# A streaming-encoder trunk: the first two weight units of a part multiplied row-wise, with a fourth weight place

## What is computed

```python
for l in range(DEPTH):
    x = layer_norm(ALPHA * x + 0.5 * swiglu(x, w_gate, w_up, w_down), ln1_g, ln1_b)   # F = 2816
    h = x @ w_in            # q, k, v of 8 stick-breaking heads, q, k, v of 8 chunked heads
    ...
    x = layer_norm(ALPHA * x + mixed @ w_out, ln2_g, ln2_b)
    x = layer_norm(ALPHA * x + 0.5 * swiglu(x, w_gate2, w_up2, w_down2), ln3_g, ln3_b)
```

## Time and profile before

| | |
|---|---|
| median of 3 runs | 1013.1 us (1012.2 to 1013.25) |
| the profiled execution's own time | 1012.61 us |
| its span, first to last instruction | 1010.8 us |
| PE busy | 997.8 us, 99% of the span |
| PEld (weight loads, beside PE) | 921.9 us, 91% |
| DVE busy | 812.4 us, 80% |
| ACT busy | 568.6 us, 56% |
| POOL busy | 26.5 us, 3% |
| HBM traffic | 185 MB, 183 GB/s |
| chain that ended last | PE 90%, DVE 5%, issue 2%, DMA 2% |

### The profile page before, as it was taken

One profiled execution on the slowest core, in us unless ns is written; L12 is line 12 of the kernel. 1 busy time (PEld: TensorE's weight loads), 2 busy tenths in 40 slices (PEclk: granted clock), 3 DMA queues, 4 the chain that ended last, 5 costly groups with the idle time before them and its releaser, 6 DMA issues.

```text
span 1010.8 us, 17930 instructions
## 1 busy us (share of the span) xinstructions
PE 997.8 (99%) x7020; PEld 921.9 (91%) x7020; DVE 812.4 (80%) x882; ACT 568.6 (56%) x616; POOL 26.5 (3%) x54
## 2 busy tenths in 40 slices
PE   6999999999999999999999999999999999999999
PEld 6899999799987999999889999997999889999997
DVE  4998885844788899886889988868457979988859
ACT  5655554557785655554465555536586756555545
POOL 2000000001100000000000000000010000000000
PEclk9999999999999999999999999999999999999999
DMA  8556545463324555464436574545523265545441
GB/s 333 207 197 251 220 172 185 160 228 127 126 83 167 209 207 212 168 219 182 176 126 208 208 290 167 210 138 198 205 84 126 87 247 196 210 177 210 169 187 59
DMA packets 34078, 185.22 MB, mean 183 GB/s; under 512 B 3824, under 2 KB 3824, under 8 KB 18928
## 3 DMA queue, kind: packets, MB, share of 16 engines
q1 hardware_dynamic: 32400, 174.60, 47.8%
q0 software_dynamic: 1488, 9.45, 2.4%
q10 hardware_dynamic: 144, 0.52, 0.2%
HBM read 183.51 MB, written 1.05 MB: 183 GB/s over the span
## 4 chain that ended last, share of the span: by engine, by line
PE 90%; DVE 5%; issue 2%; DMA 2%; ACT 1%; SPq 0%; ACTq 0%; DVEq 0%
PE bank L1064 26%; PE bank L1065 26%; PE bank L1066 26%; PE bank L1162 8%; PE bank L1126 2%; DVE w_lo L704 2%; DMA raw<-stream 2%; DVE xn L828 1%; PE bank L1119 1%; ACT w_hi L423 1%; PE bank L1308 1%; DVE soft_t L854 0%; DVE hl_lo L922 0%; ACT hl_hi L534 0%; DVE h_lo L914 0%
## 5 line engine op out<-in xcount | busy, mean ns | idle before, releaser
L1064 PE MATMUL bank<-xT_hi,w_hi 128*128 128x256 f32 x1568 | 444.7, 284 | 0.4 <-DVE w_lo L704 0.4
L1066 PE MATMUL bank<-xT_hi,w_lo 128*128 128x256 f32 x1568 | 443.9, 283 | 0.0
L1065 PE MATMUL bank<-xT_lo,w_hi 128*128 128x256 f32 x1568 | 443.9, 283 | 0.0
L704 DVE TENSOR_TENSOR w_lo<-raw,w_hi 128x2048 fp32r<-128x2048 f32 x122 | 278.5, 2290 | 73.3 <-ACT w_hi L423 73.3
L423 ACT ACTIVATE w_hi<-raw 128x2048 fp32r<-128x2048 f32 x122 | 232.7, 1911 | 130.4 <-PE bank L1066 129.2
L1064 PEld LDWEIGHTS bank<-xT_hi,w_hi 128*128 128x128 f32 x1568 | 300.7, 192 | 3.8 <-issue 0.8
L1065 PEld LDWEIGHTS bank<-xT_lo,w_hi 128*128 128x128 f32 x1568 | 300.8, 192 | 2.9
L1066 PEld LDWEIGHTS bank<-xT_hi,w_lo 128*128 128x128 f32 x1568 | 300.7, 192 | 0.0
L1064 PE MATMUL bank<-w_hi,h_hi 128*128 128x512 f32 x284 | 111.6, 393 | 0.6 <-DVE h_lo L874 0.6
L1065 PE MATMUL bank<-w_lo,h_hi 128*128 128x512 f32 x284 | 111.4, 392 | 0.0
L1066 PE MATMUL bank<-w_hi,h_lo 128*128 128x512 f32 x284 | 110.5, 389 | 0.0
(11 more groups left out here) (137 smaller groups left out, 1170.5 us busy)
## 6 DMA issues: line engine op xcount, KB each, us to landing
raw<-stream SPq DMA_DIRECT2D x110, 1024.0 KB, 4.8
raw<-stream SPq DMA_DIRECT2D x110, 512.0 KB, 4.1
lnp<-ln_gb POOLq DMA_DIRECT2D x6, 1024.0 KB, 6.0
band<-rel_band POOLq DMA_DIRECT2D x2, 1024.0 KB, 9.2
xn<-x POOLq DMA_DIRECT2D x1, 1024.0 KB, 6.7
out<-xn SPq DMA_DIRECT2D x4, 256.0 KB, 2.0
qT<-xT SPq DMA_DIRECT2D x1, 512.0 KB, 4.6
qT<-xT ACTq DMA_DIRECT2D x1, 512.0 KB, 4.8
```

Of the source, the lines that this page charges most:

```text
L704: nc.vector.tensor_tensor(w_lo[:, at(slot)], raw[:, slot, :], w_hi[:, at(slot)].bitcast(F32), ALU.subtract).then_inc(lo_ready, 1)
L1064: nc.tensor.matmul(o, w[0], x[0], start=start, stop=False, skip_group_check=again)
L1065: nc.tensor.matmul(o, w[0], x[1], start=False, stop=False, skip_group_check=again)
L1066: return nc.tensor.matmul(o, w[1], x[0], start=False, stop=stop, skip_group_check=again)
```

## The change

1. `SLOT_AT` gives four places of 2048 in `w_hi` and `w_lo`: slot 1 at 0, slot 0 at UW, slot 2 at 2 UW, and place 3, whose last 512 also serve one attention buffer (before, `sx_hi` and `sx_lo`).
2. The first two units of each part but the first of the run are split before the part begins: the first into place 3 (after an FFN) or place 1 (before the second FFN, where W_out's last unit goes to place 3), the second, from raw slot 1, into slot 0's place in two halves. `split_second_hi` and `split_second_lo` take the place of `split_first_*`, ahead of the LN. The loads' waits are as they were.
3. Both units are multiplied row-wise: x stands still, 512 columns (256 of each unit) move (`row_products`); all of token half 0, then all of half 1. The turns of half 1 stand inside half 0's products, those of half 0's first quarter inside the last y product, its second quarter's behind it. `keep_warm` is gone. `last_used` comes after half 0's products.
4. The results lie by rows: in attention q is copied to `row_out` (ACT, scaled), turned by eight transposes and copied into `qT`; in an FFN silu and gate work on halves, and h is turned by four transposes and copied into `h_pair`.
5. In those FFNs' first step the next gate and up units both come ahead of the products, and product 7 waits for the second gate.
6. LN: `x_lo` of the first two quarters ahead of the rstd steps (before, of one), and both first x_hi ahead of `rstd` of half 1. `gather` takes six additions before the gate of the last Strassen step and two behind it.
7. The last LN has no turns, x_hi or x_lo, and the load and split after the last unit are gone.

```diff
-SLOT_AT = (0, 2 * UW, UW)
+SLOT_AT = (UW, 2 * UW, 0, 3 * UW)
...
-            load(0, DEPTH * UNITS, source=DEPTH * UNITS - 1)
...
+            def split_second_hi(l, filled, after):
+                act.wait_ge(raw_ready[1], loaded(l, 1, filled))
+                act.wait_ge(unit_used, used(l, after))
+                for c, done in zip(HALVES, (first_hi, hi_ready)):
+                    nc.scalar.activation(w_hi[:, at(0, c)], raw[:, 1, c], ACT.Copy).then_inc(done, 1)
...
                 rstd(l, p, 0)
+                if count == 3 * DEPTH:
+                    rstd(l, p, 1)
+                    return
                 x_hi(count, 0)
+                x_hi(count, 1)
                 rstd(l, p, 1)
-                x_hi(count, 1)
...
+                    split_hi(l, base + 2, 2, first[2])
+                    silu_rows(r, 0, row_silu)
+                    silu_rows(r, 1, silu_done)
+                    split_hi(l, base + 3, 0, first[0] + 1, after=base + 1)
+                    first_unit_hi()
+                    act.wait_ge(row_turned, 2 * l + f)
+                    nc.scalar.activation(h_pair, bank[6][:, :].rearrange("p (c b t) -> p c b t", c=2, b=2),
+                                         ACT.Copy).then_inc(hf_done, 1)
+                    split_differences_hi(l, f, 0)
+                    act.wait_ge(row_h_done, 2 * (2 * l + f))
+                    silu(1, 2)
+                    high_h(0)
+                    split_last_parts_hi(l, f, 0)
+                    split_hi(l, base + 5, 2, first[2] + 1)
...
                 split_hi(l, base + 3 * SF + 5, 2, first[2] + 1 + SF)
+                if r < 3 * DEPTH - 2:
+                    split_hi(l, base + FFN_UNITS, 0, first[0] + FP, into=3, after=base + 3 * SF + 1)
                 act.wait_ge(hf_done, it(l, f, FP - 1) + 1)
...
-                split_first_hi(l, base + FFN_UNITS, first[0] + FP)
+                if r < 3 * DEPTH - 2:
+                    split_second_hi(l, first[1] + FP, base + 3 * SF + 3)
...
-                split_hi_at(l, ATT0 + 15)
+                split_hi(l, ATT0 + 15, 1, FILLED[ATT0 + 15], into=3, after=ATT0 + 1)
+                split_hi(l, FFN_BASE[1], 0, FILLED[FFN_BASE[1]], into=1, after=ATT0 + 12)
                 mixed_hi(l, 1, 0)
                 mixed_hi(l, 1, 1)
-                split_first_hi(l, FFN_BASE[1], FILLED[FFN_BASE[1]])
+                split_second_hi(l, FILLED[FFN_BASE[1] + 1], ATT0 + 13)
...
-                    if tb == 1:
-                        x_lo(phase(l, p + 1), (0,))
+                    if tb == 1 and phase(l, p + 1) < 3 * DEPTH:
+                        x_lo(phase(l, p + 1), (0, 1))
...
+                    weight_differences(l, f, 0, FILLED[base + 1] + 1)
+                    split_lo(l, base + 2, 2)
+                    weight_additions()
+                    gated_rows(r, 0)
+                    gated_rows(r, 1)
+                    split_lo(l, base + 3, 0)
+                    h_sums(0)
+                    split_pure_lo(l, f, 0)
+                    split_differences_lo(l, f, 0)
+                    low_h(0)
...
                 split_lo(l, base + 3 * SF + 2, 2)
+                gather(l, f, 0)
                 gated(SF, 3 * SF, bank[0])
+                gather(l, f, 1)
                 split_lo(l, base + 3 * SF + 3, 0)
-                gather(l, f, 0)
...
-                gather(l, f, 1)
                 split_lo(l, base + 3 * SF + 4, 1)
                 split_lo(l, base + 3 * SF + 5, 2)
+                last = 2 * l + f == 2 * DEPTH - 1
+                if not last:
+                    split_lo_into(l, base + FFN_UNITS, 0, 3)
                 gated(FP - 1, 3 * SF + 3, bank[4])
...
-                split_first_lo(l, 2 * f + 1, base + FFN_UNITS)
+                if not last:
+                    split_second_lo(l, 2 * f + 1, base + FFN_UNITS + 1)
...
                 mixed_lo(l, 1, 1)
-                split_lo_at(l, ATT0 + 15)
-                split_first_lo(l, 2, FFN_BASE[1])
+                split_lo_into(l, ATT0 + 15, 1, 3)
+                split_lo_into(l, FFN_BASE[1], 0, 1)
+                split_second_lo(l, 2, FFN_BASE[1] + 1)
...
+            def row_products(l, rel, tb, other, count, turn=None):
...
+                def product(x, part, kc, start=False, stop=False):
+                    return plain(o, x[:, kc, t], w[part][:, s:s + 2, c0 + kc * 256:c0 + (kc + 1) * 256], start, stop)
+                pe.wait_ge(lo_ready, split(l, rel + 1))
                 for half in range(2):
+                    pe.wait_ge(xhi_done, count * 4 + (2 * tb + half + 1))
+                    for kc in range(4 * half, 4 * half + 4):
+                        product(xT_hi, 0, kc, start=kc == 0)
+                        product(xT_hi, 1, kc)
+                for half in range(2):
+                    pe.wait_ge(xlo_done, count * 4 + (2 * tb + half + 1))
+                    if turn and half == 1:
+                        turn(0)
+                    for kc in range(4 * half, 4 * half + 4):
+                        last = product(xT_lo, 0, kc, stop=kc == KC - 1)
+                if turn:
+                    last.then_inc(row_done, 1)
+                    turn(1)
+                else:
+                    last.then_inc(unit_used, 2)
+
+            def first_pair(l, rel, other, count, units):
+                turn_x(0, count, 1)
+                row_products(l, rel, 0, other, count, lambda half: turn_x(1, count, half))
+                last_used(count - 1, units)
+                row_products(l, rel, 1, other, count)
...
+                    first_pair(l, base, 1 if f else 3, count, 2 if f else 1)
+                    columns(l, base + 2, 2, bank[0], (0,))
+                    pe.wait_ge(row_h_done, 2 * (2 * l + f))
...
+                    last.then_inc(row_turned, 1)
+                    columns(l, base + 2, 2, bank[0], (1,))
+                    columns(l, base + 3, 0, bank[7])
...
-                first_columns(l, ATT0, phase(l, 1))
-                for a in range(1, 4):
-                    w_in(l, a)
+                first_pair(l, ATT0, 3, phase(l, 1), 1)
+                w_in(l, 2, (0,))
...
+                w_in(l, 2, (1,))
+                w_in(l, 3)
...
-                turn_x(0, phase(l, 1))
-                keep_warm(4)
-                turn_x(1, phase(l, 1))
```

More of the change, by code:

```diff
@@ L295, in _, with load @@
         def _(sp):
-            def load(slot, n, back=3, source=None):
+            def load(slot, n, back=3):
                 sp.wait_ge(lo_ready, n + (4 - back))
-                fetch(slot, n if source is None else source)
+                fetch(slot, n)
             def fetch(slot, n):
@@ L415, in _, with split_hi @@
             act.dma_start(qT[:, 4:8, :], xT_in[:, 4:8, :]).then_inc(xT_loaded[1], 16)
-            def split_hi(l, rel, slot, filled):
+            def split_hi(l, rel, slot, filled, into=None, after=None):
                 act.wait_ge(raw_ready[slot], loaded(l, slot, filled))
@@ L522, in ffn @@
                     high_h(j + 1)
+                if r < 0:
+                    step(0)
+                next_unit(0)
+                with act.Fori(1, SF - 1) as j:
+                    step(j)
+                    next_unit(j)
                 step(SF - 1)
@@ L1090, in rows, with down @@
                     last.then_inc(unit_used, 1)
-            def down(slot, hi, lo, c0, tbs, start=False, stop=False, halves=(0, 1)):
+            def down(slot, hi, lo, c0, tbs, start=False, stop=False, halves=(0, 1), turn=None):
                 for tb in tbs:
@@ L1102, in down, with pair @@
                 return last
-            def pair(slot, h, tb, half, stop=False):
+            def pair(slot, h, tb, half, stop=False, turn=None):
                 for c in range(2):
+                    if c == 1 and turn:
+                        turn_x(0, turn, 0)
                     a = 2 * c + tb
@@ L1230, in ffn @@
                     for half in range(2):
-                        pair(2, hl, tb, half, True).then_inc(y_done, 1)
-                last_used(phase(l, 2 * f), 1)
+                        turn = tb == 1 and half == 1 and count + 1 < 3 * DEPTH
+                        pair(2, hl, tb, half, True, count + 1 if turn else None).then_inc(y_done, 1)
             def sb_scores(l, b):
@@ L1378, in attention @@
                         for half in range(2):
-                            last = down(SLOT[rels[i]], xT_hi, xT_lo, 2 * i, (tb,), stop=i == 3, halves=(half,))
+                            turn = (tb, i, half) == (1, 3, 1)
+                            last = down(3 if i == 3 else SLOT[rels[i]], xT_hi, xT_lo, 2 * i, (tb,), stop=i == 3,
+                                        halves=(half,), turn=phase(l, 2) if turn else None)
                             if i == 3:
                                 last.then_inc(y_done, 1)
-                last_used(phase(l, 1), 2)
             pe.wait_ge(consts, 10)
```

198 lines of the change are left out of this document (128 added, 70 removed).

## The result

| | before | after |
|---|---|---|
| median of 18 runs each, us | 1012.5 (1011.9 to 1013.3) | 1016.4 (1013.9 to 1019.7) |
| profiled execution, us (span) | 1012.6 (1010.8) | 1017.5 (1015.8) |

The ratio is 1.0040, 95% interval 1.0033 to 1.0046: slower by 0.4%, 4 us, which is more than the 0.2% that a measurement of this kernel can tell. The forecast was 1013.4, and no change was its likeliest sign; the time lies in the range, but 0.4 us above the band of the forecast (1011 to 1016), and next to the time of rival two (1017.0). The runs after also scatter over 5.8 us, those before over 1.3.

The account below looks back on a forecast made before the run. TensorE's instruction list was taken as the bound (busy 997.8 of 1010.8 us). Terms A -5.6, C -2.4, B +9.0, end -0.7 sum to +0.3, giving 1012.9 profiled and 1013.4 us median; range 1005.5 to 1018.5.

Parts of the forecast that it names:

- rival two: Both holes in B drop TensorE to its lower clock, costing 3 us each: 1017.0 us; chance 0.20.
- place A: An FFN into attention, twice: half one's products run during half two's LN; -2.8 us each, -5.6 in all.
- T0: Moment when the next part's first two units are multiplied; forecast 3.9 us earlier in A and C, 1.8 later in B.
- q's turns: Eight new turns of q in attention, place A: 0.86 + 0.2 us added.
- The expected meeting of TensorE and the third quarter of xn: Place A: TensorE finishes half one's products at 200.1, when that quarter arrives at 200.2.
- C: Layer 0's second FFN into layer 1's first, once: 3.9 us gained at T0, 1.5 lost at the FFN's start; -2.4.
- The FFN's start: First step of each later FFN: 0.85 us stall for the second gate, 1.5 us with h's turns.
- The end: Last part: late gate gone, last LN's Square no longer behind a copy; -0.7 us, between -0.2 and -1.3.
- Place B: Attention into second FFN, twice: LN waits behind the second unit's load, 5.5 us hole; +9.0 us with FFN starts and clock.
- I take 1.2 each, because LN hides a part: Clock price per hole in B: 1.2 us taken, between nothing and the run start's 3 us.
- Rival one: No hole in B, so B gains as C does: sum -13.5, 999.6 us; chance 0.14.
- Rival three: Clock holds at no cost, the rest as forecast or better: -2.1, 1011.0 us, down to 1007; chance 0.23.

Follow-up runs that it names:

- e5: e1 with VectorE's second gate ahead of the weight sums in the first step of each later FFN: 1001.9 us, ratio 0.9893.
- e4: Changed kernel, with ScalarE's two `mixed_hi` ahead of the hi split of the second FFN's first unit in place B: 1014.5 us, ratio 1.0020.
- e7: Changed kernel plus 6 filler matmuls in front of the first turn in W_out's last product, where TensorE waits: 1014.6 us, ratio 1.0019.
- e9: e6 with POOL's load of x held until four transfers into raw slot 2 have landed instead of one: 995.9 us, ratio 0.9833.
- e12: Kernel before the change, with POOL's load of x held until four transfers into raw slot 2 have landed instead of one: 1010.8 us, ratio 0.9985.
- e6: e5 with e4's edit as well: 999.0 us, ratio 0.9868.
- e8: Kernel before the change, without its filler matmuls (`keep_warm`) at all six places: 1020.5 us, ratio 1.0080.
- e10: e6 with the turn of half 0's first quarter behind the last y product instead of inside it: 1000.6 us, ratio 0.9877.
- e1: Changed kernel, with both splits of the second unit moved behind the LN of token half 0 in place B only: 1004.8 us, ratio 0.9929.

## Why the prediction was right and wrong

**What bounds it, and place A: right.** The forecast -3.9 at T0 came out at -4.05, q's turns 1.06 at 0.87, so A is -3.2 each instead of -2.8. The expected meeting of TensorE and the third quarter of xn is the 0.26 us wait. The same 4.05 stands in C. One reading was off: the list of waits before does have a hole above 0.5 us, the 0.6 us for h_lo in the first step, which is the one that grew.

**The FFN's start: right.** Forecast 1.5, measured 1.38, of which 1.1 is the wait by the list (forecast 0.85); e5 removed it by moving the gate and gave back 0.98 a place. **The end**: -0.5 against -0.7.

**Place B: right in mechanism, short by 1.6 us a place.** The hole was forecast at 5.5 and was 5.42 in the first place and 6.58 in the second, released by xn, behind a landing, with the LN late. But T0 was to be 1.8 later plus 1.2 for the clock, and was 4.49 and 4.77 later. Counted from W_out's start, the LN was forecast at 19.9 us and came at 21.4 and 21.8, so the whole miss lies ahead of the LN. Three steps failed:
- *"(slot 0, loaded long before)"*. It wasn't. The first unit's load is issued at 298.2, after W_out has begun, and lands at 304.2. ScalarE's split, now ahead of the `mixed_hi`, waited 1.19 for it; so VectorE's splits ended 1.2 later than the sum had them, the second unit's load was issued that much later (13.1 us after W_out's start against 11.9), and the LN started as much later. The first hole kept its size since TensorE itself lost 1.4 in W_out for the same reason. In the second place the wait was 0.39 and the issue 0.4 late. e4 removes this: the LN 1.8 and 1.1 us earlier.
- *"lands 4.7 us later"*. It did so before, in both places, and took 4.9 in the first place after. In the second it took 6.1 (6.0 to 6.4 in most runs of the family), 1.4 more than the sum had. Why is open: POOL has no load under way there.
- *"I take 1.2 each, because LN hides a part"*. e7 puts it at 1.6 to 1.7. The forecast chose a value between nothing and 3. From the hole's end to T0 it had 14.3 us without the clock, some 0.5 too long, which hid the difference: 15.5 us forecast with it, 15.5 and 15.4 measured. That this stretch came out is luck.

**The start: not in the prediction.** 2.5 us in the profiled pair, of which 0.9 are clock behind a longer wait; by e9 and e12 that wait comes from a collision of loads and scatters from run to run. The sum took the stretch ahead of the first changed place as equal in both kernels.

**Rival two** gave the right time, 1017.0, by a price of 3 us a hole. The price was about 1.65, and the 2.7 us less for two holes were made up by the late LN and the start. By its own words it decides "from about 2.2 us a hole on", which is where its sum, -2.1 plus two prices, passes the 2 us that can be told; at the measured price it would not have decided. It is the right sign for a reason that is half right. **Rival one**'s number was reached by e6, and the point that spoke against it, the issue right behind unit 15's split, was the one that decided. **Rival three** is excluded by the clock row.

The sum, forecast and measured: A -5.6 and -6.4; C with its start -2.4 and -2.7; B with its starts +9.0 and +12.0; end -0.7 and -0.5; run start 0 and +2.5. Forecast +0.3, measured +4.9; the median runs differ by 3.9, since this profiled execution is 1.1 above its own median.

## What to carry to other kernels

When a split or copy is moved ahead on an in-order engine, move its load's issue too, or look up when its buffer comes free: what stands behind the waiting instruction pays, not the instruction itself. Read every such load's issue and landing in the trace, the one taken for early above all. A hole of more than 3 us on TensorE cost its length here and then 1.1 to 1.7 us of clock, so put useful work in it, and filler where there is none. A hole that no edit touches can cost clock too, as in the first step: look at the granted clock behind every hole of more than 2 us before taking two profiles as alike.

## What the runs showed of the hardware

- Every hole of 3.4 us (e8) to 6.6 us (after) brought the granted clock to 0.50, the 1.2 GHz level, also the 3.7 and 4.1 us in the first step of e7 and e10. It returned 3 to 5.5 us after the hole's end, with TensorE at work. Up to 2.14 us it never fell; 2.41 us (after) did it and 2.90 us (e1) did not. The price was 0.9 (after's first step) to 1.7 us a hole. Filler kept it at 1.00 (e7).
- The fall came inside the holes of 4.7 us and more, and in e8 between 0.3 us ahead of a hole's end and 1.7 us behind it, when TensorE was at work again.
- A float32 matmul of 512 columns is two instructions of 0.43 us; the fp32r ones of the kernel are one, 0.23 apart (0.12 for 256 columns).
- A 1 MB load of weights landed 4.7 to 4.9 us after its issue at most places, 6.0 to 6.4 us in the second place B of several runs (why is open), and 6.9 (before) and 8.2 (after) beside a 1 MB load from POOL's queue, where it took 4.8 once that load was moved (e9).
